# Sample states on VectorE, a cache copy in eight pieces, and a sigmoid in two parts, in a two-layer decoder step

## The chip, the cores and the metric

The kernel runs on one core of one Trainium2 chip. The metric is device time in microseconds (us) of one execution, lower is better. The engines are TensorE (PE), VectorE (DVE), ScalarE (ACT), GpSimd (POOL) and SyncE (SP, which here only issues transfers). POOL issues transfers too, on a queue of its own. In the profile q1 carries the transfers that SP issues, q0 those of POOL.

## The reference

One inference step of a two-layer trunk, for a prompt of 256 tokens and for 8 samples of one token each, which share every weight. Layer 0 mixes tokens by an mLSTM: each of 8 heads keeps a matrix memory C of 96x96 per sample. Layer 1 uses sparse attention over a paged cache. Each layer ends in a feed-forward network, dense in layer 0, top-2 of 8 experts in layer 1. The change touches layer 0 and one copy of layer 1's cache. In the reference, with one token per sample:

```python
num = einsum('btsh,bshd->bthd', qk, vc) + g[..., None] * einsum('bhvk,bthk->bthv', C, qc)
den = sum(qk, axis=2) + g * einsum('bhk,bthk->bth', n, qc)
hc = num / maximum(abs(den), exp(-mt))[..., None]
C = gl[..., None, None] * C + einsum('bsh,bshv,bshk->bhvk', wl, vc, kc)
...
h = sigmoid(o_pre).reshape(shp) * h
h = h * rsqrt(mean(h * h, axis=-1, keepdims=True) + RMS_EPS) * head_g
...
win_s = concatenate([cache_nsa_win[li], kvs[:, :, 4:]], axis=1)[:, -wbuf:]
```

So for each sample and head the kernel needs the product of C with the query (C is 96x96), and the renewed C as an output. The last line shifts a window of 512 rows by one for each of 8 samples: 511 rows of 2048 bytes are copied from input to output unchanged, about 1 MB for each sample, 8 MB in all.

## The kernel before, in words

Every engine has its own program, written out by hand, and engines meet by semaphores (`wait_ge`). `link` (L615) makes an engine wait for its own last instruction, so VectorE's and ScalarE's work is serial. Weights stream through a ring of three slots: SP issues the load of chunk n once the readers of chunk n-3 are done (L2357 to L2366).

The part around the change is layer 0, in this order:

- **Head loop** (L2871 to L2890 on VectorE). For each of the 8 heads TensorE forms scores, VectorE subtracts and masks (`decay`, `weigh`), ScalarE takes an exponential between the two (`decayed`) and copies the head's rows out of a bank (`hp`) and the gate's preactivation (`opened`). TensorE also computes the output gate's projection for a later head (`open_gate`). `sample_rows` holds small work of the samples. In heads 2 to 5 VectorE reduces the products of the samples' states (`state_reduce`). POOL makes these products (`multiply`, L3094) from the state `cs` and query rows that a transfer has spread over 96 partitions (`widen`).
- **Gate and norm.** ScalarE takes one sigmoid over all 8 heads (2112 columns) after head 5, then `gated` multiplies and squares on VectorE (heads 0 to 5 in one piece, 6 and 7 in another), then come the denominator, the mean, a reciprocal (L2899), and a root on ScalarE. TensorE spreads the result back to the heads, and L2902 multiplies eight times.
- **Projection.** Eight tiles of the output projection on TensorE, each added to `xT` by VectorE (L2907). A norm follows (L2675 to L2687).
- **Feed-forward network.** 22 tiles; tile j needs half of weight chunk `gu{j // 2}` (two transfers of 1 MB each), which VectorE splits in two parts (`piece`, L667 and L668) two tiles ahead. The semaphore `ff_mm` counts the tiles that TensorE has done.
- **POOL**, all through that time: the products, then the renewal of the states (`update`, three operations of 96x768 a sample, L3099 to L3102), the stores of the renewed states (`keep`), and then the copy of the window's rows, in one transfer. After it POOL's program goes on with layer 1 (`layer_b_pool`), which starts with a wait for the end of the feed-forward network.

Of the kernel before, what the change touches and what calls it, by code (L numbers as in the profile page):

```python
# [9 lines left out]
ALU = mybir.AluOpType  # L10
# [18 lines left out]
WBUF = 512  # L29
# [33 lines left out]
    "parts": (("ff_sp", 30), ("m_sp", 288)),  # L63
    "hidden": (("ff_h", 22), ("m_h", 48)),
    "gated": (("ff_si", 22), ("m_si", 48)),
    "once_act": (("ms_e0", 1), ("o_si", 1), ("gates", 3), ("ms_e1", 1), ("pc_e0", 1), ("pc_te", 1), ("pc_e", 2),
                 ("cm_e0", 1), ("cm_e", 1), ("rt_e", 1), ("f_ss0", 1), ("f_ss1", 1), ("f_rs0", 1), ("f_rs1", 1), ("f_ss2", 1), ("f_rs2", 1)),
}
STAGE = {}
# [107 lines left out]
def bc(ap, axis, n):  # L177

    v = ap.unsqueeze(axis)
    shape = list(v.shape)  # L180
    shape[axis] = n
    return v.broadcast_to(tuple(shape))
# [55 lines left out]
def build(nc, I, O):  # L238
    ctx = ExitStack()
    with ctx:  # L240
# [12 lines left out]
        def S(name):  # L253

            name = STAGE.get(name, (name,))[0]
            if name not in sems:
                sems[name] = ctx.enter_context(nc.semaphore(name))
            return sems[name]

        def done(name, n=1):  # L260

            sem, before = STAGE.get(name, (name, 0))
            return S(sem), before + n
# [124 lines left out]
        def wide_heads(at):  # L388

            return at.rearrange("p (h k) -> p h k", h=MH)  # L390
# [2277 lines left out]
        def _(dve):  # L2668
# [177 lines left out]

            def state_reduce(b):

                dve.wait_ge(S("pq"), b + 1)
                link(V.tensor_reduce(r_s[:, b, :], wide_heads(q_wide[b // 2 % 2][:, b % 2, :]), AX.X, ALU.add), "rd")  # L2850

            def sample_heads():

                dve.wait_ge(*done("gb_mm"))
                link(V.tensor_copy(gb[:, 1:3, :, :].rearrange("p a b c -> p (a b c)"), bank[4][0:MD, 0:128]))
                link(V.tensor_tensor(r_s, r_s, gb[:, 1, :, :], ALU.mult))
                dve.wait_ge(S("qks_ev"), 5)
                link(V.tensor_tensor(t_s, vT.rearrange("p h b -> p b h"), gb[:, 2, :, :], ALU.mult))
                link(V.tensor_tensor(r_s, r_s, t_s, ALU.add))
                dve.wait_ge(*done("o_si"))  # L2860
                link(V.tensor_tensor(hT[:, :, TP:NT], r_s.rearrange("p b h -> p h b"), og[:, :, TP:NT], ALU.mult))
                link(V.tensor_tensor(sq[0:MD, :, TP:NT], hT[:, :, TP:NT], hT[:, :, TP:NT], ALU.mult))

# [10 lines left out]
            for h in range(MH):  # L2874
                if h + 1 < MH:
                    weigh(h + 1)
                if h < 7:
                    finish(h)
                sample_rows(h)
                if 2 <= h < 6:  # L2880
                    state_reduce(2 * h - 4)
                    state_reduce(2 * h - 3)
                if h == 6:
                    sample_heads()
                    gated(0, 6, "hsq0")
                if h == 7:
                    gated(6, 8, "hsq")
                if h + 2 < MH:
                    decay(h + 2)
# [10 lines left out]
            for h in range(MH):  # L2900
                dve.wait_ge(*done("hn_bc", h + 1))
                link(V.scalar_tensor_tensor(hT[:, h, :], hT[:, h, :], hg[:, h:h + 1], bank[head_bank[h]][0:MD, 0:NT],  # L2902
                                            ALU.mult, ALU.mult), "hn")

            for m_ in range(KT):
                dve.wait_ge(*done("woa_mm", m_ + 1))
                link(V.tensor_tensor(xT[:, m_, :], xT[:, m_, :], bank[2 + m_ % 2][:, 0:NT], ALU.add), "woa_ev")  # L2907
            def piece(n):
# [11 lines left out]
            dve.wait_ge(S("st_a"), 16)  # L2920
            dve.wait_ge(S("st_n"), 32)
            dve.wait_ge(S("st_cv"), 64)
            dve.wait_ge(S("cup"), 3 * TS)
            norm(2, xT[:, :, :], NT, uT[:, :, :], FFN0, lambda: piece(0))
            split(V, link, "u_split0", uT[:, :, :], uh, uT_r[:, :, :])
            piece(1)
# [22 lines left out]
        def _(act):  # L2949
            link = chain(act, "act")  # L2950

            def f(out, in_, fn, **kw_):
                return nc.scalar.activation(out, in_, fn, **kw_)  # L2953
# [71 lines left out]
            for h in range(MH):  # L3025
                act.wait_ge(S("nd_mm"), h + 1)
                link(f(hT[:, h, 0:TP], bank[3][0:MD, 0:TP], ACT.Copy), "hp")
                if h + 2 < MH:
                    decayed(h + 2)
                    opened(h + 2)  # L3030
                if h == 5:
                    link(f(og, og, ACT.Sigmoid), "o_si")
            act.wait_ge(*done("bd"))
            link(f(rtmp[0:MH, 0:1], over_eps, ACT.Sqrt))
            act.wait_ge(S("hn_rc"), 1)
# [13 lines left out]
        def _(pool):  # L3049
# [38 lines left out]

                load(name, dst, scr_qk[:, first:first + n, what, :].broadcast_to((MD, n, TOK)))

            def multiply(b):

                at = wide_heads(q_wide[b // 2 % 2][:, b % 2, :])
                nc.gpsimd.tensor_tensor(at, at, cs[:, b, :, :], ALU.mult).then_inc(S("pq"), 1)  # L3094

            def update(b):

                at = wide_heads(k_wide[:, b - 2, :] if 2 <= b < 7 else q_wide[1][:, b % 7, :])
                nc.gpsimd.tensor_tensor(at, at, bc(vT[:, :, b], 2, MD), ALU.mult).then_inc(S("cup"), 1)  # L3099
                nc.gpsimd.tensor_tensor(cs[:, b, :, :], cs[:, b, :, :], bc(gb[:, 0, b, :], 2, MD), ALU.mult).then_inc(S("cup"), 1)  # L3100
                pool.wait_ge(S("cup"), 3 * b + 2)
                nc.gpsimd.tensor_tensor(cs[:, b, :, :], cs[:, b, :, :], at, ALU.add).then_inc(S("cup"), 1)  # L3102

            def keep(j):

                pool.wait_ge(S("cup"), 6 * j + 6)
                store(O["C_s"][0, 2 * j:2 * j + 2].rearrange("b h v k -> v (b h) k"),
                      cs[:, 2 * j:2 * j + 2, :, :].rearrange("p b h k -> p (b h) k"), "st_c")

# [4 lines left out]
            pool.wait_ge(S("st_qk"), 16)  # L3114
            widen("ld_qa", q_wide[0], 0, 0, 2)
            widen("ld_qb", q_wide[1], 0, 2, 2)
            pool.wait_ge(S("ld_c"), 16)
            pool.wait_ge(S("ld_qa"), 16)
            multiply(0)
            multiply(1)  # L3120
            pool.wait_ge(S("ld_qb"), 16)
            multiply(2)
            multiply(3)
            pool.wait_ge(S("rd"), 2)
            widen("ld_qa", q_wide[0], 0, 4, 2)
            pool.wait_ge(S("rd"), 4)
            widen("ld_qb", q_wide[1], 0, 6, 2)
            pool.wait_ge(S("ld_qa"), 32)
            multiply(4)
            multiply(5)  # L3130
            pool.wait_ge(S("ld_qb"), 32)
            multiply(6)
            multiply(7)
            pool.wait_ge(S("rd"), 8)
            widen("ld_qb", q_wide[1], 1, 0, 2)
            pool.wait_ge(S("sc_mm"), 8)
            pool.wait_ge(S("kt_mm"), 8)
            widen("ld_qa", k_wide, 1, 2, 5)
            pool.wait_ge(*done("bT_ev"))
            pool.wait_ge(S("ld_qb"), 48)  # L3140
            update(0)
            update(1)
            keep(0)
            widen("ld_qb", q_wide[1][:, 0:1, :], 1, 7, 1)
            pool.wait_ge(S("ld_qa"), 48)
            update(2)
            update(3)
            keep(1)
            pool.wait_ge(S("c_ev"), 8)
            store(O["C_p"][0, 0].rearrange("h v k -> v h k"), cout, "st_cv")  # L3150
            store(O["n_p"][0], nout, "st_cv")
# [2 lines left out]
            store(O["m_s"][0], gs[:, 5, :], "st_n")  # L3154
            pool.wait_ge(*done("n_s"))
            store(O["n_s"][0], n0, "st_n")
            update(4)
            update(5)
            keep(2)
            update(6)  # L3160
            pool.wait_ge(S("ld_qb"), 64)
            update(7)
            keep(3)
            store(O["win_s"][0, :, 0:WBUF - 1], I["cache_nsa_win"][0, :, 1:WBUF])
            layer_b_pool(pool, load, store)
            pool.wait_ge(S("stored"), 16 * stores[0])
            for name in ("st_mem", "st_a", "st_cv", "st_n", "st_c", "st_qk", "st_rows", "st_win"):
# [29 lines left out]
```

## Time and profile before

| | us |
|---|---|
| runs shown | 2086.88, 2072.53, 2072.64 |
| their median | 2072.64 |
| the profiled execution's own time | 2084.07 |
| its span | 2082.3 |
| PE busy | 1909.1 (92%) |
| DVE busy | 1318.8 (63%) |
| ACT busy | 929.6 (45%) |
| POOL busy | 179.1 (9%) |

The span is the stretch from the first to the last instruction of the profiled execution; 1.8 us of its time lie outside of it. The profiled execution belongs with the longer of the three runs, not with the median. Line numbers (L2420) are those of the kernel. L2420 is the helper of every matmul, L2953 that of every ScalarE activation, L3051 and L3056 those of every load and store that POOL issues.

### The profile page before, as it was taken

The page shows a single profiled execution, that of the slowest core. Times are in us where ns is not written, and L with a number is a line of the kernel's source. Part 1 is how long each engine was busy: PE and PEld are TensorE (multiplying, and loading weights), DVE is VectorE, ACT ScalarE, POOL GpSimd, SP SyncE. Part 2 cuts the span into 40 slices and gives each one's busy share as a digit, 9 for nine tenths or more (in the row PEclk, how much of TensorE's full clock was granted, in tenths as well). Part 3 has the DMA queues.
Part 4 walks back from the last instruction along what each step waited for, and adds up shares of the span by engine and source line. Part 5 has one row for each costly group of instructions (what it writes and reads, how often), then busy time and mean ns, then how long its engine had stood idle before and what let it go on. Part 6 is the DMA issues. An engine that isn't in the chain of part 4 may idle for free.

```text
span 2082.3 us, 28161 instructions
## 1 busy us (share of the span) xinstructions
PE 1909.1 (92%) x10322; PEld 1532.2 (74%) x10322; DVE 1318.8 (63%) x1727; ACT 929.6 (45%) x1244; POOL 179.1 (9%) x205
## 2 busy tenths in 40 slices
PE   5999977799999999999878878999999999999994
PEld 3566646799965477777645667888888888888883
DVE  4362573578633345778642345888888888888884
ACT  0122110000001035767544314778777777777772
POOL 0000254000020000000000000111011110111001
PEclk8999888899989979999979887999999999999997
DMA  4432436555662133333379453999999999999992
GB/s 169 140 103 81 102 91 220 204 171 157 193 221 89 41 120 122 122 122 122 122 263 360 151 188 141 326 349 359 370 339 336 345 359 372 338 337 343 356 377 76
DMA packets 195829, 457.93 MB, mean 220 GB/s; under 512 B 12116, under 2 KB 77776, under 8 KB 194443
## 3 DMA queue, kind: packets, MB, share of 16 engines
q1 hardware_dynamic: 187970, 423.00, 57.5%
q0 software_dynamic: 7760, 33.65, 5.4%
q8 instruction: 58, 0.95, 0.2%
q14 instruction: 41, 0.33, 0.1%
HBM read 443.75 MB, written 21.32 MB: 223 GB/s over the span
## 4 chain that ended last, share of the span: by engine, by line
PE 71%; DVE 5%; DMA 5%; issue 2%; SPq 2%; ACT 1%; POOLq 0%; POOL 0%; DVEq 0%; ACTq 0%
PE bank L2420 65%; PE bank L2423 6%; DMA ring<-in_w_ffn_gu 2%; SPq L2287 1%; DMA arena<-in_cache_nsa 1%; DVE arena L1563 1%; ACT arena L2953 1%; DMA arena<-in_cache_nsa_win 0%; DMA ring<-in_cache_nsa 0%; DMA ring<-scr_y,mem_all 0%; DVE uT L2687 0%; DVE arena L1721 0%; DVE small L1723 0%; DMA scr_imp<-ring 0%; DVE arena L1738 0%
## 5 line engine op out<-in xcount | busy, mean ns | idle before, releaser
L2420 PE MATMUL bank<-arena_r 128*128 128x448 f32 (+2 forms) x3296 | 814.4, 361 | 29.9 <-DVE arena_r L668 13.1
L2420 PEld LDWEIGHTS bank<-arena_r 128*128 128x128 f32 x3296 | 608.6, 190 | 106.2 <-issue 28.6
L1870 DVE TENSOR_TENSOR ring_r<-ring,arena_r 128x1792 fp32r<-128x1792 f32 (+1 forms) x216 | 443.8, 2089 | 47.9 <-ACT arena_r L2953 46.5
L2953 ACT ACTIVATE arena_r<-ring 128x1792 fp32r<-128x1792 f32 (+1 forms) x216 | 370.3, 1727 | 152.7 <-PE bank L2420 133.8
L2953 ACT ACTIVATE arena<-bank 64x256 f32<-64x256 f32 (+11 forms) x403 | 171.0, 434 | 421.1 <-PE bank L2420 251.7
L2420 PE MATMUL bank<-arena 128*128 128x256 f32 (+18 forms) x1506 | 252.4, 356 | 8.2 <-ACT arena L2953 6.0
L2420 PE MATMUL bank<-ring_r,arena_r 128*128 128x448 f32 (+1 forms) x840 | 246.0, 374 | 0.0
L2420 PEld LDWEIGHTS bank<-arena 128*128 128x128 f32 (+10 forms) x1506 | 172.9, 172 | 63.7 <-issue 37.2
L2420 PEld LDWEIGHTS bank<-ring_r,arena_r 128*128 128x128 f32 x840 | 157.7, 188 | 21.7
L1870 DVE TENSOR_TENSOR arena_r<-arena,arena_r 128x1792 fp32r<-128x1792 f32 (+1 forms) x72 | 138.5, 1936 | 52.0 <-ACT arena_r L2953 50.7
L2423 PE MATMUL bank<-consts_sb,arena 128*128 128x128 f32 (+6 forms) x736 | 121.1, 296 | 35.8 <-DMA arena<-in_x_sample 10.3
L2420 PE MATMUL bank<-arena_r,ring_r 128*128 128x264 f32 x528 | 152.2, 288 | 0.0
L2420 PE MATMUL bank<-uT,ring 128*96 128x264 f32 (+3 forms) x624 | 143.6, 388 | 3.1 <-DVE mem_all L2722 1.1
L2423 PEld LDWEIGHTS bank<-consts_sb,arena 128*128 128x128 f32 (+6 forms) x736 | 88.5, 148 | 74.1 <-issue 30.2
L2953 ACT ACTIVATE arena_r<-arena 128x1792 fp32r<-128x1792 f32 (+1 forms) x72 | 116.3, 1632 | 48.0 <-PE bank L2420 35.3
L2420 PEld LDWEIGHTS bank<-uT,ring 128*96 128x96 f32 (+3 forms) x624 | 99.6, 168 | 42.6 <-issue 12.5
L2953 ACT ACT_TABLE_LOAD x55 | 70.6, 1283 | 130.8 <-DVE rtmp L2680 83.1
L2423 PE MATMUL bank<-consts_sb,ring 128*128 128x128 f32 (+2 forms) x644 | 107.0, 296 | 18.2 <-DVE arena L1563 6.0
L2423 PEld LDWEIGHTS bank<-consts_sb,ring 128*128 128x128 f32 (+2 forms) x644 | 81.9, 156 | 39.5 <-issue 12.7
L2420 PE MATMUL bank<-ring,uT 128*128 128x512 f32 (+6 forms) x304 | 104.8, 502 | 0.8 <-DVE uT L2687 0.8
L2420 PE MATMUL bank<-uT_r,arena_r 128*128 128x264 f32 x352 | 102.7, 292 | 0.0
L2420 PEld LDWEIGHTS bank<-arena_r,ring_r 128*128 128x128 f32 x528 | 101.8, 193 | 0.0
(385 smaller groups left out, 1795.5 us busy)
## 6 DMA issues: line engine op xcount, KB each, us to landing
ring<-in_w_moe_gu SPq DMA_DIRECT2D x144, 896.0 KB, 6.6
ring<-in_w_moe_d SPq DMA_DIRECT2D x60, 1024.0 KB, 5.6
ring<-in_cache_nsa SPq DMA_DIRECT2D x176, 256.0 KB, 4.4
arena<-in_w_moe_gu SPq DMA_DIRECT2D x48, 896.0 KB, 5.5
ring<-in_w_ffn_gu SPq DMA_DIRECT2D x22, 1024.0 KB, 7.7
arena<-in_cache_nsa SPq DMA_DIRECT2D x80, 256.0 KB, 6.1
ring<-in_w_in_a SPq DMA_DIRECT2D x8, 1536.0 KB, 7.2
arena<-in_w_moe_d SPq DMA_DIRECT2D x12, 1024.0 KB, 5.9
```

Source lines behind the costliest of these rows:

```text
L1563: link(V.tensor_copy(*piece(t, 1, r)), "xe1", r == 1)
L1870: V.tensor_tensor(unit_low(c), unit_slot(c), unit_high(c), ALU.subtract).then_inc(S("m_sp"), 1)
L2287: sp.dma_start(past_row(b, l), page_rows(number, 1)).then_inc(S(f"ld_g{b % 3}"), 16)
L2420: return nc.tensor.matmul(out, lhsT, rhs, start=first, stop=last, **kw_)
L2423: return nc.tensor.transpose(out, in_, ident[0:n, 0:n])
L2953: return nc.scalar.activation(out, in_, fn, **kw_)
```

## The change

Four things are changed, all in layer 0 and in POOL's program:

1. The products of the samples' states move from POOL to VectorE, in front of each reduction, in heads 2 to 5.
2. The renewal of the states moves from POOL to VectorE: `state_update` for sample 0 after the head norm, for samples 1 to 7 ahead of the evictions of projection tiles 0 to 6. POOL keeps the transfers, and stores the states two by two as they are renewed.
3. The copy of the window's rows, one transfer of 8 samples, becomes eight transfers of one sample. The first waits until 4 tiles of the feed-forward network are done, each later one for 2 tiles more.
4. The sigmoid is taken in two parts: heads 0 to 5 after head 4, heads 6 and 7 after head 5. The gating of heads 0 to 3 moves into VectorE's head 5, that of heads 4 and 5 stays in head 6.

```diff
             def state_reduce(b):
-                dve.wait_ge(S("pq"), b + 1)
-                link(V.tensor_reduce(r_s[:, b, :], wide_heads(q_wide[b // 2 % 2][:, b % 2, :]), AX.X, ALU.add), "rd")
+                if b == 0:
+                    dve.wait_ge(S("ld_c"), 16)
+                dve.wait_ge(S("ld_qb" if b // 2 % 2 else "ld_qa"), 16 * (b // 4) + 16)
+                at = wide_heads(q_wide[b // 2 % 2][:, b % 2, :])
+                link(V.tensor_tensor(at, at, cs[:, b, :, :], ALU.mult))
+                link(V.tensor_reduce(r_s[:, b, :], at, AX.X, ALU.add), "rd")
+
+            def state_update(b):
+                at = wide_heads(k_wide[:, b - 2, :] if 2 <= b < 7 else q_wide[1][:, b % 7, :])
+                link(V.tensor_tensor(cs[:, b, :, :], cs[:, b, :, :], bc(gb[:, 0, b, :], 2, MD), ALU.mult))
+                dve.wait_ge(*((S("ld_qa"), 48) if 2 <= b < 7 else (S("ld_qb"), 64 if b == 7 else 48)))
+                link(V.tensor_tensor(at, at, bc(vT[:, :, b], 2, MD), ALU.mult))
+                link(V.tensor_tensor(cs[:, b, :, :], cs[:, b, :, :], at, ALU.add), "cup")
...
-                dve.wait_ge(*done("o_si"))
+                dve.wait_ge(*done("o_si", 2))
...
+                if h == 5:
+                    dve.wait_ge(*done("o_si"))
+                    gated(0, 4, None)
                 if h == 6:
                     sample_heads()
-                    gated(0, 6, "hsq0")
+                    gated(4, 6, "hsq0")
...
+            state_update(0)
             for m_ in range(KT):
+                if m_ < TS - 1:
+                    state_update(m_ + 1)
                 dve.wait_ge(*done("woa_mm", m_ + 1))
...
-            dve.wait_ge(S("cup"), 3 * TS)
...
-                if h == 5:
-                    link(f(og, og, ACT.Sigmoid), "o_si")
+                if h in (4, 5):
+                    some = og[:, 0:6, :] if h == 4 else og[:, 6:8, :]
+                    link(f(some, some, ACT.Sigmoid), "o_si")
...
-                pool.wait_ge(S("cup"), 6 * j + 6)
+                pool.wait_ge(S("cup"), 2 * j + 2)
...
-            keep(3)
-            store(O["win_s"][0, :, 0:WBUF - 1], I["cache_nsa_win"][0, :, 1:WBUF])
+            pool.wait_ge(S("cup"), 1)
+            widen("ld_qb", q_wide[1][:, 0:1, :], 1, 7, 1)
+            for j in range(TS // 2):
+                keep(j)
+            for b in range(TS):
+                pool.wait_ge(*done("ff_mm", 2 * b + 4))
+                store(O["win_s"][0, b, 0:WBUF - 1], I["cache_nsa_win"][0, b, 1:WBUF])
```

VectorE's program in head 5, before (-) and in the change (+). L2853 is a product, L2854 its reduction, L2880 and L2881 are `gated`, and L2796 and L2797 are `decay` for head 7, on which ScalarE's last exponential waits.

```order
-L2850 TENSOR_REDUCE arena<-mem_all 96x8 x2
+L2853 TENSOR_TENSOR mem_all<-mem_all,arena 96x768
+L2854 TENSOR_REDUCE arena<-mem_all 96x8
+L2853 TENSOR_TENSOR mem_all<-mem_all,arena 96x768
+L2854 TENSOR_REDUCE arena<-mem_all 96x8
+L2880 TENSOR_TENSOR arena<-arena 96x4x256
+L2881 TENSOR_TENSOR arena<-arena 96x4x256
 L2796 TENSOR_SCALAR arena<-bank,arena 128x256
 L2797 TENSOR_SCALAR arena<-bank,arena 128x128
```

Two products and two gating operations now stand ahead of the last `decay`.

ScalarE's program before, from the exponential of head 7 (128x384) to the root after the loop; 96x2112 is the sigmoid.

```order
L2953 ACTIVATE arena<-arena 128x384
L2953 ACTIVATE arena<-bank 96x264
L2953 ACT_TABLE_LOAD
L2953 ACTIVATE arena<-arena 96x2112
L2953 ACTIVATE arena<-bank 96x256 x2
L2953 ACT_TABLE_LOAD
```

And in the change, from the exponential of head 6; 96x1584 and 96x528 are the two parts of the sigmoid.

```order
L2970 ACTIVATE arena<-arena 128x384
L2970 ACTIVATE arena<-bank 96x264
L2970 ACT_TABLE_LOAD
L2970 ACTIVATE arena<-arena 96x1584
L2970 ACTIVATE arena<-bank 96x256
L2970 ACT_TABLE_LOAD
L2970 ACTIVATE arena<-arena 128x384
L2970 ACTIVATE arena<-bank 96x264
L2970 ACT_TABLE_LOAD
L2970 ACTIVATE arena<-arena 96x528
L2970 ACTIVATE arena<-bank 96x256 x2
L2970 ACT_TABLE_LOAD
```

The exponential of head 7 now stands between the two parts of the sigmoid, and a table load stands ahead of each of the three.

POOL's program at the end of layer 0, before:

```order
L3099 TENSOR_TENSOR mem_all<-mem_all,arena 96x768
L3100 TENSOR_TENSOR arena<-arena 96x768
L3102 TENSOR_TENSOR arena<-arena,mem_all 96x768
L3056 DMA out_C_s<-arena 96x16x96
L3056 DMA out_win_s<-in_cache_nsa_win 8x16x16352
L3051 DMA arena<-in_b_gate_b 128x36
```

And in the change, the same place:

```order
L3069 DMA mem_all<-scr_qk 96x768
L3074 DMA out_C_s<-arena 96x16x96 x4
L3074 DMA out_win_s<-in_cache_nsa_win 16x16352 x8
L3069 DMA arena<-in_b_gate_b 128x36
```

The copy's outermost dimension was 8; each of the eight pieces has 16 as its outermost dimension, in rows of 16352 numbers. TensorE's and SP's programs are the same in both kernels.

## Rows read from the trace of the kernel before

**Rows 1.** The page: chain of waits that ended last, by line.
```profile
PE bank L2420 65%; PE bank L2423 6%; DMA ring<-in_w_ffn_gu 2%; SPq L2287 1%; DMA arena<-in_cache_nsa 1%; DVE arena L1563 1%; ACT arena L2953 1%; DMA arena<-in_cache_nsa_win 0%; DMA ring<-in_cache_nsa 0%; DMA ring<-scr_y,mem_all 0%; DVE uT L2687 0%; DVE arena L1721 0%; DVE small L1723 0%; DMA scr_imp<-ring 0%; DVE arena L1738 0%
```
**Rows 2.** The chain in order of time: start, duration, what.
```profile
338.27 49.53 DMA ring<-in_w_ffn_gu
```
**Rows 3.** Timeline of VectorE around the third feed-forward tile: start, busy, engine, line, operation.
```profile
387.93 1.23 DVE L667 CAST arena_r<-ring 128x2048 fp32r<-128x2048 f32 x1 [19.09 <-DMA ring<-in_w_ffn_gu]
```
**Rows 4.** Timeline of ScalarE: its activation that follows each feed-forward tile.
```profile
379.89 0.39 ACT L2953 ACTIVATE arena<-bank 128x264 f32<-128x264 f32 x1 [4.17 <-PE bank L2420]
401.47 0.39 ACT L2953 ACTIVATE arena<-bank 128x264 f32<-128x264 f32 x1 [21.19 <-PE bank L2420]
407.32 0.39 ACT L2953 ACTIVATE arena<-bank 128x264 f32<-128x264 f32 x1 [5.46 <-PE bank L2420]
```
**Rows 5.** Timeline of POOL: the issue of the copy.
```profile
336.71 0.65 POOL L3056 DMA_DIRECT2D out_win_s<-in_cache_nsa_win  x1
```
**Rows 6.** Transfers: issues with KB each and median us to landing.
```profile
ring<-in_w_ffn_gu SPq DMA_DIRECT2D x22, 1024.0 KB, 7.7
out_win_s<-in_cache_nsa_win POOLq DMA_DIRECT2D x1, 8176.0 KB, 46.0
```
**Rows 7.** Transfers from 350 to 380 us: queue, packets, MB, share of 16 engines.
```profile
q0 software_dynamic: 96, 6.28, 49.3%
q1 hardware_dynamic: 96, 0.10, 0.9%
```
**Rows 8.** Timeline of VectorE in the head loop.
```profile
245.86 2.18 DVE L2831 TENSOR_TENSOR ring<-arena 8x768 f32<-8x768 f32 x1
253.87 0.94 DVE L2834 TENSOR_TENSOR ring<-arena 8x768 f32<-8x768 f32 x1
258.85 0.29 DVE L2806 TENSOR_TENSOR arena<-arena,consts_sb 128x128 f32<-128x128 f32 x1
265.38 2.10 DVE L2806 TENSOR_TENSOR arena<-arena,consts_sb 128x128 f32<-128x128 f32 x1
269.98 1.47 DVE L2839 TENSOR_TENSOR arena<-arena 8x8 f32<-8x8 f32 x1
271.90 0.16 DVE L2842 TENSOR_TENSOR arena<-arena 8x8 f32<-8x8 f32 x1
```
**Rows 9.** Timeline of VectorE between the loop and the root.
```profile
285.94 1.75 DVE L2868 TENSOR_TENSOR arena<-arena 96x1536 f32<-96x1536 f32 x1
289.52 1.86 DVE L2868 TENSOR_TENSOR arena<-arena 96x512 f32<-96x512 f32 x1
294.96 1.59 DVE L2894 TENSOR_TENSOR arena<-arena 8x256 f32<-8x256 f32 x1
299.09 1.79 DVE L2899 RECIPROCAL arena<-arena 8x264 f32<-8x264 f32 x1
```
**Rows 10.** Timeline of ScalarE at heads 6 and 7.
```profile
281.06 0.52 ACT L2953 ACTIVATE arena<-arena 128x384 f32<-128x384 f32 x1 [4.20 <-DVE arena L2797]
282.03 1.28 ACT L2953 ACT_TABLE_LOAD   x1
```
**Rows 11.** Timeline of TensorE before and in the projection.
```profile
301.54 7.32 PE L2420 MATMUL bank<-arena,consts_sb 8*96 8x264 f32 x16 [7.18 <-ACT arena L2953]
308.79 5.88 PE L2420 MATMUL bank<-arena,ring 96*128 96x264 f32 x16
315.40 3.73 PE L2420 MATMUL bank<-arena,ring 96*128 96x264 f32 x16
```
**Rows 12.** Stretches: us, busy of PE, PEld, DVE, ACT, POOL, granted clock, DMA share, GB/s.
```profile
302.00:309.00 7.00, 7.00 (x17) 4.10 (x16) 3.42 (x8) 0.00 (x0) 6.92 (x5) 0.50 0.41 106
317.00:330.00 13.00, 13.00 (x60) 11.09 (x59) 1.29 (x3) 0.00 (x0) 12.30 (x9) 1.00 0.54 132
```
**Rows 13.** Timeline of VectorE: evictions of the projection's first two tiles.
```profile
315.67 0.43 DVE L2907 TENSOR_TENSOR xT<-xT,bank 128x264 f32<-128x264 f32 x1 [6.22 <-PE bank L2420]
320.12 0.43 DVE L2907 TENSOR_TENSOR xT<-xT,bank 128x264 f32<-128x264 f32 x1 [4.02 <-PE bank L2420]
```

More of the change, by code:

```diff
@@ L65 @@
     "gated": (("ff_si", 22), ("m_si", 48)),
-    "once_act": (("ms_e0", 1), ("o_si", 1), ("gates", 3), ("ms_e1", 1), ("pc_e0", 1), ("pc_te", 1), ("pc_e", 2),
+    "once_act": (("ms_e0", 1), ("o_si", 2), ("gates", 3), ("ms_e1", 1), ("pc_e0", 1), ("pc_te", 1), ("pc_e", 2),
                  ("cm_e0", 1), ("cm_e", 1), ("rt_e", 1), ("f_ss0", 1), ("f_ss1", 1), ("f_rs0", 1), ("f_rs1", 1), ("f_ss2", 1), ("f_rs2", 1)),
@@ L3089, in widen @@
                 load(name, dst, scr_qk[:, first:first + n, what, :].broadcast_to((MD, n, TOK)))
[L3091 to L3102, printed above, removed]
             def keep(j):
-                pool.wait_ge(S("cup"), 6 * j + 6)
+                pool.wait_ge(S("cup"), 2 * j + 2)
                 store(O["C_s"][0, 2 * j:2 * j + 2].rearrange("b h v k -> v (b h) k"),
@@ L3116, in _ @@
             widen("ld_qb", q_wide[1], 0, 2, 2)
[L3117 to L3123, printed above, removed]
             pool.wait_ge(S("rd"), 2)
@@ L3127, in _ @@
             widen("ld_qb", q_wide[1], 0, 6, 2)
[L3128 to L3133, printed above, removed]
             pool.wait_ge(S("rd"), 8)
@@ L3138, in _ @@
             widen("ld_qa", k_wide, 1, 2, 5)
[L3139 to L3148, printed above, removed]
             pool.wait_ge(S("c_ev"), 8)
@@ L3156, in _ @@
             store(O["n_s"][0], n0, "st_n")
[L3157 to L3162, printed above, removed]
-            keep(3)
-            store(O["win_s"][0, :, 0:WBUF - 1], I["cache_nsa_win"][0, :, 1:WBUF])
+            pool.wait_ge(S("cup"), 1)
[5 more added lines that the diff above has]
+                store(O["win_s"][0, b, 0:WBUF - 1], I["cache_nsa_win"][0, b, 1:WBUF])
             layer_b_pool(pool, load, store)
```

## The prediction

> **What bounds the kernel now.** I read the chain of waits first. It is TensorE's for 71% of the span, nearly all in one matmul line, and the only transfer with more than 1% is the load of the feed-forward weights [rows 1]. In order of time that transfer is one piece: a weight chunk, on its way from 338.3 us for 49.5 us [rows 2], where the median of its 22 kind is 7.7 us [rows 6]. VectorE stands idle for 19.1 us until it lands [rows 3]. Then I looked for what the transfer shared the queues with: POOL had issued the 8 MB copy 1.6 us earlier, at 336.7 [rows 5], and the copy took 46.0 us to land [rows 6]. From 350 to 380 us POOL's queue moved 96 packets of 65 KB and SP's queue also exactly 96, of 1 KB; together the 16 engines were about half busy [rows 7]. The reader is to see that half of the engines carry the copy and let one small weight packet through for each large one. A copy packet costs 0.493 x 16 x 30 / 96 = 2.46 us of an engine. The copy is 8176 KB / 65.4 KB = 128 packets, 16 on each of eight engines: 39.4 us, near the 46.0 measured. Before all this, from about 240 to 301 us, VectorE is the serial engine of the head loop and of the gate, with hardly a gap, and some of its rows are long only while POOL computes [rows 8, 9].
>
> **The copy in pieces.** ScalarE follows each feed-forward tile. Tiles stand 5.85 us apart (401.47 to 407.32), but the second and third stand 21.58 apart (379.89 to 401.47) [rows 4]. The excess, 15.7 us, is the whole price of the late chunk, TensorE's slow restart with it. A piece now starts when SP issues the load of a later chunk, and that chunk is wanted three tiles, 17.6 us, after its issue. If a piece lies on eight engines as the copy did, it has 2 packets an engine, 4.9 us; 7.7 + 4.9 = 12.6 us, inside 17.6. If it lies on sixteen it is 2.5 us. I take it as hidden; the cover is the 17.6 us. All of POOL's later work waits for the end of the feed-forward network, so its waits hold up nobody. Gain 15.7 us. Below that is nothing (pieces slow the chunks as the copy did), above it nothing, since tiles at 5.85 us are TensorE's own.
>
> How a single sample's copy spreads over the engines no row shows; the change gives it an outermost dimension of 16 where the old one had 8. The Trainium skill (DMA: Bandwidth & Descriptors, "Why a DMA increments its semaphore by 16 and not by 1") says that the slowest dimension sets the number of engines, at most 16. By that rule a piece has one packet on each engine; the old copy's half share of the engines agrees with it. The sum would be the same, and the slow rival below would be impossible.
>
> **Products on VectorE.** Eight products of 768 columns. A two-input operation of 768 columns takes 0.94 us undisturbed [rows 8], 0.98 with the wait between: +7.8 us, all on the path, since VectorE is the serial engine there. Query rows that POOL loads after each pair of reductions have a head or more to land, so I expect no wait for them.
>
> **POOL's arithmetic goes.** In the head loop five VectorE rows are long while POOL computes: 2.18 and 1.47 us and the mask's 2.10 are shown, where the like take 0.94, 0.16 and 0.29 [rows 8]; two more are 1.51 and 1.21. Together they lose 6.6 us. After the loop the 512-column pieces take 1.86 us against 1.75 for 1536 columns, and the 256-column step 1.59 [rows 9]; five such rows lose 5.8 us against the price by columns. Both are on the path, and both vanish if POOL is the cause. Bounds: none of it or all of it, 0 to -12.4. I take all, since the same mask takes 0.29 or 2.10 us in one loop [rows 8].
>
> **The gate in parts.** Gating heads 0 to 3 is 1024 columns twice, 1.17 us each by 1.75 for 1536 [rows 9], 2.4 us. It moves, it adds nothing. The exponential of head 7 now comes after a sigmoid, so a table load of 1.28 us [rows 10] stands between VectorE's `decay` and its `weigh`: +1.3 us on the path. The first part of the sigmoid, a load and 1584 columns, some 2.8 us, lies beside VectorE's long head 5. In turn VectorE reaches the last gating earlier than TensorE has head 7 (some 0.8 us of wait), and the mean later waits for TensorE some 0.7: +1.5 us. What the one big sigmoid held up before was next to nothing.
>
> So up to head 7's `decay`: +7.8 + 2.4 - 6.6 = +3.6. From there to the end of the reciprocal: -5.8 - 2.4 + 1.3 + 1.5 = -5.4. Both: -1.8 us.
>
> **TensorE's clock.** It stands idle for 7.2 us before the spreading matmuls; these take 7.32 us and the first projection tile 5.88 us, where a later one takes 3.73 [rows 11]. The granted clock is 0.50 (1.2 GHz) from 302 to 309 us and 1.00 (2.4 GHz) from 317 [rows 12]. With VectorE's path shorter from head 7 to the root I work out a gap of about 3 us, and expect some of that stretch at the high level. At the high level throughout it would give back 2.1 us in the tile and up to 3 in the spreading. Bounds 0 to -5, I take -3.
>
> **Renewal on VectorE.** 24 operations of 768 columns at 0.98 us are 2.9 us a sample. Two samples, 5.9 us, stand before the first eviction, where VectorE had 6.2 us idle; one before each of the next six, where it had 4.0 [rows 13]. If the clock is up sooner, the first gap shrinks and that eviction is some 2 us late; TensorE has two banks and does not wait for it. Nothing is late for the norm. Cover gone, each sample would cost up to 2.9 us. I cost it at 0.
>
> **Sum.** -15.7 - 1.8 - 3.0 = -20.5. Against the profiled execution's own 2084.07: **2063.5 us**. That execution is 11.4 us above the median of the runs shown, 2072.64; the forecast is 9.1 us, 0.4%, below the median.
>
> **The rivals.**
>
> *The median was made without the stall.* The runs are 2072.5, 2072.6 and 2086.9, with 2084.1 profiled: two groups 11.4 to 14.3 us apart, about the 15.7 us of the late chunk. The chunk was issued only 1.1 us after POOL's copy; were TensorE 3 us earlier or POOL later, it would be most of the way in. Then what is to be had against 2072.6 is the other 4.8 us: 2067.8. This nearly coincides with the sum, as it should if the groups have this cause. I keep both as one case, 2060 to 2070, chance 0.60.
>
> *The two groups have another cause*, and the stall is in all of them: 2072.6 - 20.5 = 2052.1. For it: nothing in the rows shows that the stall varies. Against: the sizes agree. Chance 0.17.
>
> *VectorE's head loop grows.* The products cost 7.8 us, and the long rows are not POOL's doing, or the loads of query rows come late. With none of the 12.4 us given back: 2063.5 + 12.4 = 2075.9; with half, 2069.7. Against: the pairs of like rows. Chance 0.16.
>
> *The pieces lie on one engine each*, slower. Place: weight chunks 4 to 10 of the feed-forward network, each behind a piece of 16 packets on one engine, with one small packet let through for each. 16 x 2.46 = 39.4 us, and 7.7 + 39.4 = 47.1 against the 17.6 of cover: 29.5 us late. It decides once a piece has more than (17.6 - 7.7) / 2.46 = 4 packets on one engine. One late chunk would give 2093; with three slots in the ring every third pays, some 88 us, 2152. For it: the chunk in the trace did wait for the copy's engines. Against: the outermost dimension of 16 and the half share of the engines under 8. Chance 0.04. The last 0.03 is for what I have not seen.
>
> **How the numbers follow.** The time is that of the likeliest case, rounded: 2064. The range takes in the other cause at 2052 and reaches up over half of the head-loop case and the lower bounds of the clock: 2051 to 2074. A measurement of this kernel can tell about 1%, 20.7 us, from no change: faster means below 2051.9, slower above 2093.4. Only half of the second case lies near or below the first bound, with a little for two gains at once: faster 0.12. Slower 0.05 is the last rival and the unseen. The rest, 0.83, lies between.
>
> **What would show it.** Right: no weight chunk over 15 us to landing; feed-forward tiles 5.85 us apart from the first on; no VectorE mask over 0.4 us; head 7's `weigh` some 2 us behind its `decay`; evictions of the projection less than 5 us apart. Wrong: VectorE waiting for feed-forward weights with a piece under way; waits for query rows in heads 4 and 5; TensorE waiting for an eviction in the projection; long rows on VectorE with POOL at rest.

## The result and the profile after

| | us |
|---|---|
| before, median of 20 runs (the 3 shown and 17 more) | 2075.91 |
| changed, median of 20 runs | 2062.90 |
| ratio, 95% interval | 0.9927, 0.9912 to 0.9941 |
| changed, profiled execution and its span | 2060.21, 2058.4 |

The change makes the kernel 0.7% faster: 15.1 us by the ratio, 13.0 by the two medians. More runs moved the median of before from 2072.64 to 2075.91, and the 20 runs fill the stretch from 2067 to 2087 us without a gap of more than 3.6 us: the two groups that the prediction saw in four numbers do not show.

The chain of waits by line, in the changed kernel:

```profile
PE bank L2420 67%; PE bank L2423 6%; SPq L2287 1%; DMA arena<-in_cache_nsa 1%; DVE arena L1563 1%; ACT arena L2970 1%; DVE uT L2687 0%; DMA arena<-in_cache_nsa_win 0%; DMA ring<-in_cache_nsa 0%; DMA ring<-scr_y,mem_all 0%; DVE rtmp L2680 0%; DVE arena L1721 0%; DMA scr_imp<-ring 0%; DVE small L1723 0%; DVE arena L1738 0%
```

Against [rows 1] the load of feed-forward weights has left the chain. ScalarE behind the second and third feed-forward tile:

```profile
377.20 0.40 ACT L2970 ACTIVATE arena<-bank 128x264 f32<-128x264 f32 x1 [4.18 <-PE bank L2420]
383.04 0.39 ACT L2970 ACTIVATE arena<-bank 128x264 f32<-128x264 f32 x1 [5.45 <-PE bank L2420]
```

They stand 5.84 us apart, where [rows 4] has 21.58. The transfers (KB each, median us to landing), and then POOL's queue from 389 to 400 us, in which one piece moves, and from 392 to 395 us (packets, MB, share of 16 engines):

```profile
ring<-in_w_ffn_gu SPq DMA_DIRECT2D x22, 1024.0 KB, 7.3
out_win_s<-in_cache_nsa_win POOLq DMA_DIRECT2D x8, 1022.0 KB, 8.9
...
q0 software_dynamic: 32, 1.05, 22.3%
...
q0 software_dynamic: 13, 0.85, 66.4%
```

22.3% of 16 engines for 11 us is 39.2 us for 1.05 MB; the copy before had 6.28 MB for 237 [rows 7], the same price by byte. From 392 to 395 us its packets take 0.664 x 16 x 3 = 31.9 us, which is more than ten engines' worth, so a piece lies on more engines than the copy did. The longest landing of one of these weight transfers is 12.2 us, inside the 17.6 us of cover. VectorE in the head loop and up to the end of the reciprocal:

```profile
248.71 0.32 DVE L2811 TENSOR_SCALAR arena<-bank,arena 128x96 f32<-128x96 f32 x1 [1.20 <-issue]
...
250.71 0.95 DVE L2853 TENSOR_TENSOR ring<-ring,arena 96x768 f32<-96x768 f32 x1
...
265.20 0.30 DVE L2806 TENSOR_TENSOR arena<-arena,consts_sb 128x128 f32<-128x128 f32 x1
...
285.06 0.56 DVE L2805 TENSOR_TENSOR arena<-arena,bank 128x384 f32<-128x384 f32 x1 [1.98 <-issue]
...
291.42 0.69 DVE L2880 TENSOR_TENSOR arena<-arena 96x512 f32<-96x512 f32 x1 [1.12 <-ACT arena L2970]
...
293.76 0.41 DVE L2909 TENSOR_TENSOR arena<-arena 8x256 f32<-8x256 f32 x1
...
296.55 0.42 DVE L2913 SCALAR_TENSOR_TENSOR arena<-bank,arena 8x264 f32<-8x264 f32 x1 [1.48 <-PE bank L2420]
297.00 1.79 DVE L2914 RECIPROCAL arena<-arena 8x264 f32<-8x264 f32 x1
```

The rows that were long beside POOL's arithmetic in [rows 8] and [rows 9] are short: the mask takes 0.30 us instead of up to 2.10, a gating operation of 512 columns 0.69 instead of 1.86, the step of 256 columns 0.41 instead of 1.59. In their place stand new waits: 1.20 us, 1.98 for the last exponential and the table load ahead of it, 1.12 for head 7 and 1.48 for the mean. TensorE after that, VectorE's first evictions of the projection, and the granted clock in three stretches (the number ahead of the DMA share):

```profile
299.46 6.79 PE L2420 MATMUL bank<-arena,consts_sb 8*96 8x264 f32 x16 [3.02 <-ACT arena L2970]
306.18 5.82 PE L2420 MATMUL bank<-arena,ring 96*128 96x264 f32 x16
```
```profile
313.00 0.43 DVE L2925 TENSOR_TENSOR xT<-xT,bank 128x264 f32<-128x264 f32 x1 [0.22 <-PE bank L2420]
317.45 0.43 DVE L2925 TENSOR_TENSOR xT<-xT,bank 128x264 f32<-128x264 f32 x1 [1.05 <-PE bank L2420]
```
```profile
294.00:300.00 6.00, 2.98 (x14) 1.25 (x13) 3.22 (x6) 0.42 (x1) 2.35 (x4) 1.00 0.24 54
300.00:310.00 10.00, 10.00 (x24) 6.51 (x23) 6.90 (x12) 0.00 (x0) 0.00 (x0) 0.50 0.00 0
305.00:312.00 7.00, 7.00 (x20) 4.98 (x20) 6.00 (x9) 0.00 (x0) 0.55 (x1) 0.63 0.08 20
```

TensorE's gap is 3.0 us instead of 7.2, and yet its matmuls are hardly faster than in [rows 11]. The clock stood at the high level through the gap (1.00 up to 300 us) and fell to 0.50 just after the matmuls had begun; it was up again only behind 310 us. The renewals fit: VectorE still waits 0.22 and 1.05 us for the tiles, 4.45 us apart as before.

The same places in both traces, in us:

| stretch | before | after | |
|---|---|---|---|
| start to the end of head 2's `decay` (nothing changed yet) | 239.92 | 237.07 | -2.9 |
| from there to the end of head 7's `decay` | 41.05 | 46.01 | +5.0 |
| to the end of the reciprocal | 19.91 | 15.71 | -4.2 |
| to the first eviction of the projection | 14.79 | 14.21 | -0.6 |
| to the third feed-forward tile | 85.80 | 70.04 | -15.8 |
| to the end of the span | 1680.83 | 1675.36 | -5.5 |

The four rows in which something changed give -15.6 us, near the 15.1 of the ratio. The first and the last, -8.4 us together, belong to these two executions.

### The profile page after: what moved, and what is told of

Its sections match the earlier page's. It is cut to its first block, busy times and chain, and to the rows that moved or that the text cites. A ratio compares the mean times of both kernels' runs of the same rounds, so it can differ in the third digit from the quotient of the medians.

```text
span 2058.4 us, 28180 instructions
## 1 busy us (share of the span) xinstructions
PE 1896.0 (92%) x10322; PEld 1522.1 (74%) x10322; DVE 1337.0 (65%) x1761; ACT 931.9 (45%) x1247; POOL 134.8 (7%) x180
## 4 chain that ended last, share of the span: by engine, by line
PE 73%; DVE 6%; issue 3%; DMA 2%; SPq 2%; ACT 1%; POOLq 0%; POOL 0%; DVEq 0%; ACTq 0%
PE bank L2420 67%; PE bank L2423 6%; SPq L2287 1%; DMA arena<-in_cache_nsa 1%; DVE arena L1563 1%; ACT arena L2970 1%; DVE uT L2687 0%; DMA arena<-in_cache_nsa_win 0%; DMA ring<-in_cache_nsa 0%; DMA ring<-scr_y,mem_all 0%; DVE rtmp L2680 0%; DVE arena L1721 0%; DMA scr_imp<-ring 0%; DVE small L1723 0%; DVE arena L1738 0%
## 5 line engine op out<-in xcount | busy, mean ns | idle before, releaser
L2420 PEld LDWEIGHTS bank<-arena_r 128*128 128x128 f32 x3296 | 607.8, 189 | 94.4 <-issue 15.4
L1870 DVE TENSOR_TENSOR ring_r<-ring,arena_r 128x1792 fp32r<-128x1792 f32 (+1 forms) x216 | 443.4, 2087 | 48.0 <-ACT arena_r L2970 46.6
```

The lines of the kernel that those rows point to most:

```text
L1870: V.tensor_tensor(unit_low(c), unit_slot(c), unit_high(c), ALU.subtract).then_inc(S("m_sp"), 1)
L2420: return nc.tensor.matmul(out, lhsT, rhs, start=first, stop=last, **kw_)
```

## The experiments

I held two theories. **A**: the weight chunk behind the copy is the whole gain. **B**: VectorE's moves and the clock give a good part, as I had forecast (4.8 us). Within A there are two readings: what counts is the engines that the copy keeps to itself (A1), or that the copy runs while the chunk is wanted (A2). The runs lie on three chips, each kernel beside the kernel before on its chip:

| run | median us | before, same chip | ratio, 95% interval |
|---|---|---|---|
| `e1_one_copy` | 2072.10 | 2079.26 | 0.9965, 0.9947 to 0.9983 |
| `e2_pieces_only` | 2063.49 | 2079.26 | 0.9931, 0.9909 to 0.9952 |
| `e3_sixteen` | 2064.45 | 2079.26 | 0.9923, 0.9894 to 0.9951 |
| `e5_two_samples` | 2140.76 | 2079.26 | 1.0304, 1.0268 to 1.0339 |
| `e4_sigmoid_whole` | 2054.55 | 2081.21 | 0.9880, 0.9846 to 0.9914 |
| `e6_products_pool` | 2054.17 | 2081.21 | 0.9878, 0.9843 to 0.9913 |
| `e7_products_pool_sigmoid_whole` | 2049.92 | 2081.21 | 0.9857, 0.9823 to 0.9891 |
| `e8_gate_after_decay` | 2054.87 | 2081.21 | 0.9882, 0.9837 to 0.9926 |
| `e9_change_again` | 2063.71 | 2081.50 | 0.9926, 0.9898 to 0.9955 |
| `e10_pieces_again` | 2064.96 | 2081.50 | 0.9939, 0.9914 to 0.9964 |
| `e11_best_again` | 2049.87 | 2081.50 | 0.9866, 0.9834 to 0.9898 |

### The copy, alone and undone

`e1_one_copy`, from the changed kernel:

```diff
-            for b in range(TS):
-                pool.wait_ge(*done("ff_mm", 2 * b + 4))
-                store(O["win_s"][0, b, 0:WBUF - 1], I["cache_nsa_win"][0, b, 1:WBUF])
+            store(O["win_s"][0, :, 0:WBUF - 1], I["cache_nsa_win"][0, :, 1:WBUF])
```

> The changed kernel, with the copy of the window's rows again in one transfer of 8 samples, at its old place behind the last store of the states. Theory A, the weight chunk that stood behind the copy is the whole gain: the second and third feed-forward tiles stand 21.6 us apart again, one weight transfer takes 45 to 50 us to land, and the time goes back by 15.7 us, to 2078 or 2079, no better than the kernel before. Theory B, a good part of the gain (4.8 us, as I forecast) is VectorE's and the clock's: the time is 2071, some 5 us under the kernel before.

ScalarE behind tiles 4 and 5, VectorE's wait ahead of tile 5, and the late chunk in the chain of waits (start, us):

```profile
387.91 0.39 ACT L2970 ACTIVATE arena<-bank 128x264 f32<-128x264 f32 x1 [5.46 <-PE bank L2420]
405.78 0.39 ACT L2970 ACTIVATE arena<-bank 128x264 f32<-128x264 f32 x1 [17.47 <-PE bank L2420]
```
```profile
393.23 1.23 DVE L667 CAST arena_r<-ring 128x2048 fp32r<-128x2048 f32 x1 [12.19 <-DMA ring<-in_w_ffn_gu]
...
345.31 47.80 DMA ring<-in_w_ffn_gu
```

The stall is back, but two tiles later and smaller: 17.87 - 5.85 = 12.0 us. The copy is issued 4.5 us later here (341.2 us), so the chunk that stood behind it gets ahead of it, and the next one is caught instead. This kernel keeps 0.35% over the kernel before (7.3 us), not the nothing that theory A foretold: 3.7 us of it is the smaller stall, and the other half I can't place. So the price of the copy depends on which chunk it meets. It does not vanish when a chunk slips past, as my first rival had it.

`e2_pieces_only`, from the kernel before, is the same edit the other way round:

```diff
-            store(O["win_s"][0, :, 0:WBUF - 1], I["cache_nsa_win"][0, :, 1:WBUF])
+            for b in range(TS):
+                pool.wait_ge(*done("ff_mm", 2 * b + 4))
+                store(O["win_s"][0, b, 0:WBUF - 1], I["cache_nsa_win"][0, b, 1:WBUF])
```

> The kernel before with one edit: the copy in eight pieces, each behind a count of feed-forward tiles, as in the change. Products, renewal and sigmoid as before. Theory A: all tiles from the first on 5.85 us apart, 15.7 us under the kernel before, 2060, the same as the whole change. Theory B: 2060 plus 4.8, since what VectorE and the clock give is missing: it stays 2065 or more. In the trace the products and the reciprocal stand where they stood before.

0.9931 against 0.9927 for the whole change. The intervals alone would leave room for some 5 us either way; the traces don't. From the end of head 2's `decay` to the third feed-forward tile its trace has 146.0 us, the changed kernel's 146.0, the kernel before 161.6. The second traces of both kernels (`e9`, `e10`) have 146.0 again. The copy is the whole gain in this stretch, and everything else in the change nets nothing there. Theory B is out.

### How many engines the copy lies on

`e3_sixteen`, from the kernel before:

```diff
-            store(O["win_s"][0, :, 0:WBUF - 1], I["cache_nsa_win"][0, :, 1:WBUF])
+            whole = (O["win_s"][0, :, 0:WBUF - 1], I["cache_nsa_win"][0, :, 1:WBUF])
+            store(*(t.rearrange("b r k g d -> b (r k g d)").rearrange("b (a c) -> a b c", a=16) for t in whole))
```

> The kernel before with one edit: the copy stays one transfer at its old place, but its outermost dimension is the 16 parts of a sample's rows instead of the 8 samples. Theory A1, what counts is the engines that the copy keeps to itself: it lies on all 16, with 8 packets each, 8 x 2.46 = 19.7 us; it lands in 22 to 28 us, the chunk issued beside it at about the same time, before it is wanted at 374, and the 15.7 us are had without any move. Theory A2, what counts is that the copy runs while the chunk is wanted, wherever it lies: the chunk waits for the whole copy, lands after 380 and stops VectorE as before.

The copy's landing; POOL's queue from 346 to 362 us; and VectorE's wait for the chunk with ScalarE behind tile 3:

```profile
out_win_s<-in_cache_nsa_win POOLq DMA_DIRECT2D x1, 8176.0 KB, 30.4
...
q0 software_dynamic: 78, 5.10, 97.2%
```
```profile
372.69 1.23 DVE L667 CAST arena_r<-ring 128x2048 fp32r<-128x2048 f32 x1 [7.04 <-DMA ring<-in_w_ffn_gu]
```
```profile
376.33 0.39 ACT L2953 ACTIVATE arena<-bank 128x264 f32<-128x264 f32 x1 [4.18 <-PE bank L2420]
383.81 0.39 ACT L2953 ACTIVATE arena<-bank 128x264 f32<-128x264 f32 x1 [7.08 <-PE bank L2420]
```

One transfer, at its old place, now keeps nearly all 16 engines busy. A packet takes 0.972 x 16 x 16 / 78 = 3.19 us in this stretch, somewhat more than the 2.46 of [rows 7]. It lands in 30.4 us, not the 22 to 28 expected, and the chunk beside it is 1.6 us late at tile 3 (7.48 instead of 5.85) instead of 15.7. The ratio is that of the eight pieces. A1 holds: a change of the shape alone brings nearly the whole gain, with no transfer moved. How many bytes a copy has, and when it runs, did not have to change.

`e5_two_samples`, from the changed kernel:

```diff
-            for b in range(TS):
+            for b in range(0, TS, 2):
                 pool.wait_ge(*done("ff_mm", 2 * b + 4))
-                store(O["win_s"][0, b, 0:WBUF - 1], I["cache_nsa_win"][0, b, 1:WBUF])
+                store(O["win_s"][0, b:b + 2, 0:WBUF - 1], I["cache_nsa_win"][0, b:b + 2, 1:WBUF])
```

> The changed kernel, with the eight pieces as four transfers of two samples, behind 4, 8, 12 and 16 feed-forward tiles. The outermost dimension of each is 2. Theory A1, engines: each transfer puts 16 packets of 2.46 us on each of two engines, 39.4 us, lands in about 45, and the weight chunk issued beside it takes about 47 us instead of 7; it is wanted after 17.6, so each such meeting costs up to 29.5 us: at least 29.5 in all, up to 118, the time 2092 to 2181. Theory A2, bytes alone: 2 MB of copy delay a chunk by some 11.5 us, 7.7 + 11.5 = 19.2 us, and cost under 2 us each: 2070 at most.

POOL's queue from 392 to 412 us, where one transfer is under way, and from 415 to 425 us, where two are; waits of VectorE from 380 to 600 us (total, times, longest); and ScalarE behind tiles 8 to 11:

```profile
q0 software_dynamic: 253, 0.98, 12.1%
...
q0 software_dynamic: 16, 1.05, 24.1%
```
```profile
DVE arena_r L667 <- DMA ring<-in_w_ffn_gu: 84.8, 4, 30.8
```
```profile
412.67 0.39 ACT L2970 ACTIVATE arena<-bank 128x264 f32<-128x264 f32 x1 [5.46 <-PE bank L2420]
448.14 0.39 ACT L2970 ACTIVATE arena<-bank 128x264 f32<-128x264 f32 x1 [35.08 <-PE bank L2420]
453.98 0.39 ACT L2970 ACTIVATE arena<-bank 128x264 f32<-128x264 f32 x1 [5.45 <-PE bank L2420]
471.05 0.39 ACT L2970 ACTIVATE arena<-bank 128x264 f32<-128x264 f32 x1 [16.68 <-PE bank L2420]
```

One transfer takes 12.1% of the 16 engines, two take 24.1%: two engines each. The transfers land in 33.6 us in the median, not the 45 expected; the chunk that meets the first takes 45.8, near the 47 expected. The first meeting costs 35.47 - 5.85 = 29.6 us, where 29.5 was worked out from 16 packets on one engine and 17.6 us of cover. The four waits are not alike. They come in two pairs, 29.6 and 11.2 us, then 30.7 and 10.8 us (the tiles stand 35.47, 17.07, 36.54 and 16.66 us apart there), 82.3 us in all, and the kernel is 78 us slower than the changed one. This is the prediction's slow rival: its price for one late chunk was right. How many chunks would pay was worked out there for eight pieces, and four transfers don't test it. What kept it away is the 16 in the outermost dimension. The same bytes, in fewer transfers on fewer engines, are 3% slower than the kernel before.

### The sigmoid, the products, the gating

The two stretches for these kernels, from the end of head 2's `decay` (us). In the second traces of the change, of `e7` and of `e2` the sums come out again within 0.1 us:

| | to head 7's `decay` | to the reciprocal's end | both | against the change |
|---|---|---|---|---|
| changed | 46.0 | 15.7 | 61.7 | |
| `e4_sigmoid_whole` | 43.5 | 15.3 | 58.8 | -2.9 |
| `e6_products_pool` | 43.3 | 15.5 | 58.8 | -2.9 |
| `e7`, both | 40.8 | 14.9 | 55.7 | -6.0 |
| `e8_gate_after_decay` | 43.5 | 15.4 | 58.9 | -2.8 |
| `e2_pieces_only` | 40.8 | 19.9 | 60.7 | -1.0 |

`e4_sigmoid_whole`, from the changed kernel:

```diff
-                if h in (4, 5):
-                    some = og[:, 0:6, :] if h == 4 else og[:, 6:8, :]
-                    link(f(some, some, ACT.Sigmoid), "o_si")
+                if h == 5:
+                    link(f(og, og, ACT.Sigmoid), "o_si")
...
-                if h == 5:
-                    dve.wait_ge(*done("o_si"))
-                    gated(0, 4, None)
...
-                    gated(4, 6, "hsq0")
+                    gated(0, 6, "hsq0")
```

> The changed kernel with the sigmoid in one piece after head 5 and the gating of heads 0 to 5 in head 6, as before the change; the rest as changed. Theory, the split costs more than it gives: VectorE's way to head 7's decay is 2.5 us shorter and the table load before the last exponential is gone (1.3 us), the wait for head 7 and a part of that for the mean go too. From the decay of head 3 to the end of the reciprocal 3 us less than in the changed kernel's trace. Rival, the split hid the sigmoid: VectorE then waits 1 to 2 us for it in the samples' gating and the stretch is no shorter. On the clock both are hard to see: 2060 against 2063.

2.9 us, as expected. The split of the sigmoid is a loss: it buys two table loads, one on the path, and what it hides is small. With the sigmoid whole VectorE waits 0.47 us for it, where the rival had 1 to 2.

`e6_products_pool`, from the changed kernel, with POOL's eight multiplications among its `widen` loads as in the kernel before:

```diff
             def state_reduce(b):
-                if b == 0:
-                    dve.wait_ge(S("ld_c"), 16)
-                dve.wait_ge(S("ld_qb" if b // 2 % 2 else "ld_qa"), 16 * (b // 4) + 16)
+                dve.wait_ge(S("pq"), b + 1)
                 at = wide_heads(q_wide[b // 2 % 2][:, b % 2, :])
-                link(V.tensor_tensor(at, at, cs[:, b, :, :], ALU.mult))
                 link(V.tensor_reduce(r_s[:, b, :], at, AX.X, ALU.add), "rd")
...
+                nc.gpsimd.tensor_tensor(at, at, cs[:, b, :, :], ALU.mult).then_inc(S("pq"), 1)
```

> The changed kernel with the products back on POOL; renewal stays on VectorE. Theory, VectorE's rows beside POOL's arithmetic are long because of it: four or five rows of the head loop are long again, 5 to 7 us in all, against 7.9 us of products saved; from the decay of head 3 to that of head 7 some 2.5 us less than in the changed kernel's trace, and no long row after the loop, since POOL has no renewals there. Rival, long rows are VectorE's own: they do not come back in the loop, and the stretch is 7.9 us shorter. Time 2060, or 2055 by the rival.

VectorE's mask in its loop, two heads:

```profile
256.83 0.29 DVE L2806 TENSOR_TENSOR arena<-arena,consts_sb 128x128 f32<-128x128 f32 x1
...
264.05 2.09 DVE L2806 TENSOR_TENSOR arena<-arena,consts_sb 128x128 f32<-128x128 f32 x1
```

Five long rows are back in the loop (1.34, 2.18, 2.09, 1.08 and 1.47 us, against 0.95, 0.94, 0.30, 0.15 and 0.15 in the changed kernel), none after it. POOL's products are their cause, and the 2.7 us between the two loops are what the products cost VectorE beyond what the quiet gives it.

`e7_products_pool_sigmoid_whole` is both edits together:

```diff
+                dve.wait_ge(S("pq"), b + 1)
-                link(V.tensor_tensor(at, at, cs[:, b, :, :], ALU.mult))
...
+                if h == 5:
+                    link(f(og, og, ACT.Sigmoid), "o_si")
```

> Both of the former edits together: products on POOL, sigmoid in one piece, with the renewals on VectorE and the copy in eight pieces as changed. If the two savings add, the stretch from head 3's decay to the end of the reciprocal is 5 to 6 us shorter than in the changed kernel's trace and the time is 2057; this would be the best version so far. If the savings have the same cover, it is 3 us.

The savings add: 6.0 us in the stretch, and 2049.92 us. This kernel also prices the renewals. It differs from `e2_pieces_only` by the renewals alone: the loop is 40.8 us in both, and the way to the reciprocal's end is 14.9 instead of 19.9. So the long rows behind the loop are the price of POOL's renewals, and their move gives 5.0 us. The change gave this away again: 2.7 us for the products, 2.9 for the split.

`e8_gate_after_decay`, from the changed kernel:

```diff
-                if h == 5:
-                    dve.wait_ge(*done("o_si"))
-                    gated(0, 4, None)
...
                 if h + 2 < MH:
                     decay(h + 2)
+                if h == 5:
+                    dve.wait_ge(*done("o_si"))
+                    gated(0, 4, None)
```

> The changed kernel with the gating of heads 0 to 3 behind head 7's decay instead of ahead of it. Theory: VectorE's idle 1.98 us before weighing head 7 (table load and exponential) is filled with 2.5 us of gating, and the stretch to the end of the reciprocal is 2.0 us shorter. Rival: TensorE's head 7 and the mean set the end of that stretch, and the waits of 1.1 and 1.5 us grow by what is saved; then it is under 1 us shorter. Time within 2 us of the changed kernel.

2.8 us shorter, more than the 2.0 expected. The gating fills VectorE's wait, and the wait for head 7 falls from 1.12 to 0.56 us, that for the mean from 1.48 to 1.17, where the rival had them grow. With the split kept, this order takes back what `e4` takes back without it.

The times of these four kernels are a miss. I expected 2060, 2060, 2057 and about 2063; they came 5 to 8 us lower. By the ratio `e4`, `e6` and `e8` stand 9 to 10 us under the change and `e7` some 15, where their stretches give 2.8 to 2.9 and 6.0. They have 4 to 6 runs each and no run of the change on their chip. Where the rest comes from stays open.

### The three versions on one chip

`e9_change_again` is the changed kernel, `e10_pieces_again` is `e2_pieces_only`, `e11_best_again` is `e7`, each unaltered.

> The changed kernel unaltered, to stand beside the next two on one chip. Theory, the copy is the gain: 15 us under the kernel before and level with the pieces alone. Rival, the moves on VectorE gave some of it unseen: 3 us or more under the pieces alone.

> The kernel before with the copy in eight pieces only. Theory: 15 us under the kernel before, within 2 us of the changed kernel. From the last decay to the end of the reciprocal 19.9 us, with POOL's renewals beside it.

> Products on POOL, sigmoid in one piece, renewals on VectorE, copy in eight pieces. The renewals alone stand between this and the pieces alone: POOL no longer computes beside the gate, 14.9 us there against 19.9, so 5 us under the pieces alone; and 6 us under the changed kernel by the two stretches of the loop and the gate.

The change and the pieces alone are level (2063.71 and 2064.96; ratios to before 0.9926 and 0.9939, intervals overlapping). The third version is 13.8 us under the change, more than the 6 expected, and 15.1 us under the pieces alone, where 5 was expected; by the ratios to before these are 0.6% and 0.7%, and the intervals touch for the first and lie apart for the second. The profiled executions of the change and of the third version lie 9.9 us apart. Of these 6.1 are in the stretch (61.7 and 55.7 us again), 2.6 ahead of it, where nothing that VectorE does has changed, 0.5 from there to the third feed-forward tile and 0.7 behind it. So 6 us are this version's doing, seen twice; for the rest I can't show that.

## Why the prediction was right, and where it was not

It said 2064, and 2062.9 was measured. It had forecast 9 us less than the median of the runs shown; the ratio gives 15.1. The direction and the main term hold. That the time was met within 1.1 us is luck, as the point on the base shows. Point by point:

- **The copy in pieces, -15.7.** Measured -15.8 in the stretch with the third feed-forward tile. `e2` shows that it is the whole gain. (The first two tiles stand 4.6 us apart in both kernels, not the 5.85 "from the first on".) The engines per transfer are as `e3` and `e5` say. The rule of the Trainium skill (DMA: Bandwidth & Descriptors, "Why a DMA increments its semaphore by 16 and not by 1"), that the outermost dimension sets how many engines carry a transfer, fits all four shapes run here: 49.3% of 16 engines with 8 before, more than ten engines at once with 16 in the pieces, 97.2% with 16 in `e3`, and 12.1% with 2 in `e5`.
- **Products, +7.8.** Eight rows of 0.95 us with their waits, 7.9.
- **POOL's rows, -12.4.** All long rows vanished; `e6` brought those of the loop back, and `e2` beside `e7` shows those behind it to be the renewals' (5.0 us). But 1.2 us of it turned into a wait for TensorE at 248.7 us, and the quiet price of the small steps was too low: 0.69 and 0.41 us, where I had worked out 0.62 and 0.33.
- **The gate in parts, +2.8.** The table load cost what I said (1.98 us of wait instead of 0.7). The waits for head 7 and the mean came to 2.6 us, not 1.5. Loop and gate together: +0.8 us instead of -1.8. The split as a whole costs 2.9 us by `e4`, near the 2.8 foreseen; what went wrong beside it is the 1.2 us of the point above.
- **The clock, -3.0: this step failed.** I read the shorter gap rightly, 3.0 us, and concluded that the matmuls behind it would find the high level. They took 6.79 and 5.82 us, 0.6 us less in all. In the kernel before the clock was low (0.50) from 296 us, ahead of the spreading matmuls, to 313; in the changed kernel it was high through the gap and low from 300 to 310 us. So the fall came behind the gap, and the rise some 10.6 us after the matmuls had begun, where it was 11.5 before. The step took the gap's length for what sets the level, and the traces don't bear that out. What does set it stays open.
- **Renewals, 0.** Right: no tile waited.
- **The base.** I made the sum against an execution of 2084.1 us. It stood 8 us above what proved to be the kernel's median, and I trusted the two groups to make up for that. My sum of -20.5 was 5 us too large, and the base 8 us too high: 2084.1 - 15.6 would have been 2068.5, and 2075.9 - 15.6 is 2060.3. Two errors of opposite sign made the number closer than the sum behind it.
- **The first rival** (the median was made without the stall), which carried the likeliest case with its 0.60, is refuted in two points: 20 runs show no two groups, and `e1` shows that a chunk ahead of the copy leaves a stall of 12.0 us behind it, not nothing. How much of the spread of the kernel before comes from the stall is open; it has one trace.

## What to carry to other kernels

Before moving or splitting a large transfer, look at its outermost dimension. In this kernel, with 8 there, 8 MB kept half of the engines busy for 40 us and let one small packet of the other queue through for each of 65 KB; with 16 the same transfer, at the same place, cost 1.6 us instead of 15.7. Work that leaves GpSimd for VectorE costs its time there less what VectorE's neighbours were slowed, so take first the part that has idle time to go to (the renewals, 5.0 us gained) and leave the part on the serial path (the products, 2.7 us lost). Putting a sigmoid ahead of an exponential cost a table load each way here, 1.28 us each.

## What the runs showed of the hardware beyond that

The granted clock makes identical work take different times. The 128 matmuls that open layer 1, of one program in both kernels, in the chain of the kernel before and then of the changed one, with the stretch's mean granted clock:

```profile
601.38 17.17 PE bank L2420 x128
...
601.40:618.60 17.20, 17.20 (x131) 15.38 (x132) 2.52 (x7) 2.00 (x4) 3.95 (x6) 0.70 0.99 345
```
```profile
581.70 14.32 PE bank L2420 x128
...
581.70:596.00 14.30, 14.30 (x130) 12.71 (x131) 2.54 (x7) 2.00 (x4) 3.95 (x6) 0.88 0.99 332
```

2.85 us apart, at a mean clock of 0.70 and 0.88, though TensorE is idle for 0.79 us ahead of them in both. The clock falls 1.7 and 5.0 us after they begin, and stays at 0.50 for some 10 us in the first trace and 3.4 in the second. This is not chance from one execution to the next: the same 128 matmuls take 17.17 us in all five traces of the kernel before, `e1`, `e2`, `e3` and `e10`, and 14.13 to 14.33 us in the other eight. It goes with the kernel, then, though nothing was changed there. Why is not shown.

Other differences are chance. `e2_pieces_only` and `e10_pieces_again` are one kernel: from the third feed-forward tile to the end their traces have 1685.4 and 1675.7 us, most of it between 700 and 1000 us, where the mean granted clock is 0.90 and 0.93. So 10 us of this kernel's spread lie where nothing was changed, and an edit of 3 us is read here from a stretch of two traces, which came out again within 0.1 us, and not from medians of six runs.
